# Five summed pairs per chunk instead of four in the up projection of a float32 decoder layer, one weight sum by accumulating DMA

## The reference

```
D_MODEL, SEQ, D_FF, FFN_RES_WEIGHT = 2048, 256, 5632, 0.5

def swiglu(x, wg, wu, wd):
    return (jax.nn.silu(x @ wg) * (x @ wu)) @ wd

f = swiglu(rmsnorm(h, ffn1_pre_g[l]), ffn1_wg[l], ffn1_wu[l], ffn1_wd[l])
h = h + FFN_RES_WEIGHT * rmsnorm(f, ffn1_post_g[l])
u = rmsnorm(h, mix_pre_g[l])
proj = u @ w_in[l]
...
h = h + rmsnorm(mixed, mix_post_g[l])
f = swiglu(rmsnorm(h, ffn2_pre_g[l]), ffn2_wg[l], ffn2_wu[l], ffn2_wd[l])
h = h + FFN_RES_WEIGHT * rmsnorm(f, ffn2_post_g[l])
```

## Time and profile before

| | |
|---|---|
| median of three runs | 2065.04 us (2064.78 to 2065.18) |
| profiled execution | span 2063.8 us, first to last instruction; no other time of this execution is given |
| TensorE busy | 2050.5 us, 99% of the span |
| VectorE busy | 1813.9 us, 88% |
| ScalarE busy | 1152.8 us, 56% |
| GpSimd busy | 27.7 us, 1% |
| granted TensorE clock | 0.999 of full speed over the span |
| DMA | 409.51 MB, 198 GB/s; loads on SyncE's queue take 60.4% of the 16 engines' time |

### The profile page before, as it was taken

One profiled execution on the slowest core, in us unless ns is written; L12 is line 12 of the kernel. 1 busy time (PEld: TensorE's weight loads), 2 busy tenths in 40 slices (PEclk: granted clock), 3 DMA queues, 4 the chain that ended last, 5 costly groups with the idle time before them and its releaser, 6 DMA issues.

```text
span 2063.8 us, 26172 instructions
## 1 busy us (share of the span) xinstructions
PE 2050.5 (99%) x9238; PEld 1694.8 (82%) x9238; DVE 1813.9 (88%) x2227; ACT 1152.8 (56%) x1292; POOL 27.7 (1%) x54
## 2 busy tenths in 40 slices
PE   9999999999999999999999999999999999999998
PEld 8888888888888788888788888888888888888886
DVE  7999999999888858998687566879999999999797
ACT  6565665566555554444466444565656565665463
POOL 0000000000000000100000000000000000000000
PEclk9999999999999999999999999999999999999999
DMA  8666656655666666776555566566666666646564
GB/s 327 222 207 203 202 187 212 211 164 177 201 194 205 187 186 192 208 202 183 178 169 181 181 191 213 183 233 201 198 205 208 198 203 201 206 143 207 198 208 163
DMA packets 211996, 409.51 MB, mean 198 GB/s; under 512 B 15113, under 2 KB 15377, under 8 KB 211520
## 3 DMA queue, kind: packets, MB, share of 16 engines
q1 hardware_dynamic: 209904, 401.26, 60.4%
q0 software_dynamic: 1856, 7.01, 1.5%
q10 hardware_dynamic: 144, 0.04, 0.0%
HBM read 406.14 MB, written 2.11 MB: 198 GB/s over the span
## 4 chain that ended last, share of the span: by engine, by line
PE 98%; DVE 1%; ACT 0%; issue 0%; DMA 0%; POOL 0%; DVEq 0%; SPq 0%; ACTq 0%; POOLq 0%
PE banks L1731 96%; PE banks L1781 2%; DVE wlo L1059 0%; DVE res L1114 0%; DMA raw<-in_ffn_wg_dram 0%; DVE h_lo L1349 0%; ACT act_hi L579 0%; DVE act_lo L1127 0%; ACT h_hi L767 0%; POOL stat L476 0%; ACT comb L683 0%; DVE comb L1083 0%; ACT junk L644 0%; ACT whi L564 0%; PE banks L2028 0%
## 5 line engine op out<-in xcount | busy, mean ns | idle before, releaser
L564 ACT ACTIVATE whi<-raw 128x1024 fp32r<-128x1024 f32 x579 | 597.8, 1052 | 490.2 <-PE banks L1731 298.3
L1059 DVE TENSOR_TENSOR wlo<-raw,whi 128x1024 fp32r<-128x1024 f32 x580 | 690.6, 1217 | 154.4 <-ACT whi L564 152.2
L1731 PE MATMUL banks<-whi,act_hi 128*128 128x512 f32 x1568 | 507.8, 395 | 0.7 <-DVE wlo L1059 0.7
L1731 PE MATMUL banks<-whi,act_lo 128*128 128x512 f32 x1568 | 498.2, 389 | 0.0
L1731 PE MATMUL banks<-wlo,act_hi 128*128 128x512 f32 x1568 | 485.2, 389 | 0.3 <-DVE wlo L1059 0.3
L1731 PEld LDWEIGHTS banks<-whi,act_lo 128*128 128x128 f32 x1568 | 294.3, 188 | 62.1
L1731 PEld LDWEIGHTS banks<-wlo,act_hi 128*128 128x128 f32 x1568 | 294.3, 188 | 62.0 <-DVE wlo L1059 0.7
L1731 PEld LDWEIGHTS banks<-whi,act_hi 128*128 128x128 f32 x1568 | 291.1, 188 | 62.5 <-issue 4.7
L564 ACT ACTIVATE whi<-raw_deep 128x1024 fp32r<-128x1024 f32 x176 | 183.0, 1054 | 172.4 <-DVE raw_deep L1259 156.3
L1059 DVE TENSOR_TENSOR wlo<-raw_deep,whi 128x1024 fp32r<-128x1024 f32 x176 | 207.8, 1220 | 7.0 <-ACT whi L564 6.9
L1731 PE MATMUL banks<-whi,h_hi 128*128 128x512 f32 x536 | 172.9, 390 | 0.5 <-ACT whi L564 0.5
(11 more groups left out here) (305 smaller groups left out, 2392.6 us busy)
## 6 DMA issues: line engine op xcount, KB each, us to landing
raw<-in_ffn_wd_dram SPq DMA_DIRECT2D x176, 512.0 KB, 4.7
raw<-in_w_in_dram SPq DMA_DIRECT2D x160, 512.0 KB, 3.6
raw<-in_ffn_wg_dram SPq DMA_DIRECT2D x88, 512.0 KB, 3.7
raw_deep<-in_ffn_wg_dram SPq DMA_DIRECT2D x88, 512.0 KB, 3.7
raw<-in_ffn_wu_dram SPq DMA_DIRECT2D x88, 512.0 KB, 4.7
raw_deep<-in_ffn_wu_dram SPq DMA_DIRECT2D x88, 512.0 KB, 4.5
raw<-in_w_out_dram SPq DMA_DIRECT2D x32, 512.0 KB, 4.1
raw<-in_w_pw_dram SPq DMA_DIRECT2D x16, 512.0 KB, 4.0
```

Of the source, the lines that this page charges most:

```text
L564: nc.scalar.activation(whi[:, j % RING, 0:kts * width], src[:, 0:kts * width], ACT.Copy).then_inc(hi_ready, 1)
L1059: nc.vector.tensor_tensor(wlo[:, j % RING, 0:n], raw_slot(j, deep)[0][:, 0:n], whi[:, j % RING, 0:n], ALU.subtract).then_inc(lo_ready, 1)
L1731: return nc.tensor.matmul(o, a, b, **kw)
```

## The change

1. `SEVEN` becomes (1, 2, 3, 5, 6): pair 2 of each summed chunk is a summed pair too. With it come a fifth activation sum per FFN and a fifth set of weight sums per chunk.
2. In the up projection b12+b22 is no longer made by VectorE. GpSimd waits for the slab of `wu` to land and issues a DMA that reads its second row block from DRAM once more and adds it to the first in place (`pair_sums`, `accum_op=ALU.add`, 256 KB). ScalarE's high part of slab 2q+1 and VectorE's sums wait for that DMA (`pair_added`).
3. The weight sums, with other signs, are b11-(b12+b22) in one instruction, and both other tiles (that plus b21, that plus b22) in one instruction of 128x1024 (`sums_of_lower_rows`). In the down projection b12+b22 stays on VectorE and now comes first; ScalarE waits for that one alone.
4. In chunks 1 to 10 the low parts of both slabs of a pair are one instruction of 128x2048 (`lo_pair`) that waits for both high parts.
5. GpSimd's program holds the fifty DMAs of an FFN's up projection ahead of the load of the gains (`load_gpost`) of FFN 1 and behind it in FFN 2.

```
-SEVEN = (1, 3, 5, 6)
+SEVEN = (1, 2, 3, 5, 6)
-P_SUM, R_SUM, Z_SUM = range(3)
+Z_SUM, P_SUM, R_SUM = range(3)
...
+            def pair_sums(f):
+                def one(c, group):
+                    for q in SEVEN:
+                        slab, full = raw_slot(2 * q + 1, True)
+                        pool.wait_ge(full, 16 * loads_in_up(f, c, 2 * q + 1))
+                        pool.dma_start(slab[:, 0:CW], rows(w_up[f][1])[:, 2 * q + 1, bass.ts(c, CW)],
+                                       accum_op=ALU.add).then_inc(added(f, c, q)[0], 16)
+                summed_chunks(pool.Fori, one)
...
                         hi_at(2 * q)
                         if q in SEVEN:
-                            act.wait_ge(wsum_ready, 4 * seven + 3)
+                            act.wait_ge(*added(f, c, q))
                         hi_at(2 * q + 1)
...
+            def lo_pair(j, ready):
+                dve.wait_ge(hi_ready, ready)
+                s = j % RING
+                src = raw[:, s:s + 2, :] if j % DEEP < RING else raw_deep[:, s:s + 2, :]
+                nc.vector.tensor_tensor(wlo[:, s:s + 2, :], src, whi[:, s:s + 2, :], ALU.subtract).then_inc(lo_ready, 2)
...
-                    nc.vector.tensor_tensor(wsum[:, P_SUM, :], b11, b12, ALU.add).then_inc(wsum_ready, 1)
+                    nc.vector.tensor_tensor(b12, b12, b22, ALU.add).then_inc(wsum_ready, 1)
                     dve.wait_ge(wsum_ready, 4 * seven + 1)
-                    nc.vector.tensor_tensor(wsum[:, R_SUM, :], wsum[:, P_SUM, :], b22, ALU.add).then_inc(wsum_ready, 1)
-                    nc.vector.tensor_tensor(b12, b12, b22, ALU.add).then_inc(wsum_ready, 1)
+                    nc.vector.tensor_tensor(wsum[:, R_SUM, :], b11, b12, ALU.subtract).then_inc(wsum_ready, 1)
                     dve.wait_ge(wsum_ready, 4 * seven + 2)
-                    nc.vector.tensor_tensor(wsum[:, Z_SUM, :], wsum[:, R_SUM, :], b21, ALU.add).then_inc(wsum_ready, 1)
+                    sums_of_lower_rows(n - 1, deep).then_inc(wsum_ready, 2)
+
+                def up_weight_sums(c, q, seven, opens):
...
+                    b11, b21, b12q, b22 = halves
+                    dve.wait_ge(*added(f, c, q))
+                    nc.vector.tensor_tensor(wsum[:, R_SUM, :], b11, b12q, ALU.subtract).then_inc(wsum_ready, 2)
+                    dve.wait_ge(wsum_ready, 4 * seven + 2)
+                    sums_of_lower_rows(2 * q, True).then_inc(wsum_ready, 2)
...
-                        for j in 2 * q, 2 * q + 1:
-                            lo(j, n0 + j + 1, deep=True)
+                        lo_pair(2 * q, n0 + 2 * q + 2)
```

More of the change, by code:

```diff
@@ L266, in build @@
             sem("wsum_ready"), sem("wsumhi_ready"), sem("wsumlo_ready"), sem("wsum_used"))
+        pair_added = [sem(f"pair_added{i}") for i in range(RING)]
         outer_copied, combined, silu_ready, hidden_ready = (
@@ L345, in summed_chunks, with added @@
             one(SUMMED, 0)
+        def added(f, c, q):
+            i = (2 * q + 1) % DEEP // 2
+            per_chunk = sum((2 * n + 1) % DEEP // 2 == i for n in SEVEN)
+            so_far = sum((2 * n + 1) % DEEP // 2 == i for n in SEVEN if n <= q)
+            return pair_added[i], 16 * (per_chunk * SUMMED * f + per_chunk * (c - 1) + so_far)
         def raw_slot(j, deep):
@@ L481, in _ @@
             root(1, rstd)
-            pool.wait_ge(mm_done, UP_SLABS)
+            def pair_sums(f):
[6 more added lines that the diff above has]
+                summed_chunks(pool.Fori, one)
+            pair_sums(0)
             load_gpost(f1_post)
@@ L541, in _ @@
             root(7, rstd)
+            pair_sums(1)
             root(8, rpost[0])
@@ L736, in quad @@
                     if q in SEVEN_OF[half]:
-                        act.wait_ge(wsum_ready, 4 * seven + 3)
+                        act.wait_ge(wsum_ready, 4 * seven + 1)
                     hi_at(n + 1)
@@ L1219, in act_sums @@
                     link(nc.vector.tensor_tensor(asum[:, i, S5, :], a21, a22, ALU.subtract))
[L1220 removed]
+                    nc.vector.tensor_tensor(asum[:, i, S7, :], a21, a11, ALU.subtract)
                     link(nc.vector.tensor_tensor(asum[:, i, S6, :], asum[:, i, S5, :], a11, ALU.subtract))
@@ L1244, in hidden, with sums_of_lower_rows @@
                     ins.then_inc(hidden_ready, 1)
+                def sums_of_lower_rows(n, deep):
+                    s = n % DEEP if deep else n % RING
+                    two = raw[:, s:s + 2, CW:2 * CW] if s < RING else raw_deep[:, s - RING:s - RING + 2, CW:2 * CW]
+                    return nc.vector.tensor_tensor(wsum[:, Z_SUM:P_SUM + 1, :], wsum[:, R_SUM:R_SUM + 1, :].to_broadcast([P, 2, CW]),
+                                                   two, ALU.add)
                 def weight_sums(seven, loads, j, opens, deep=False):
@@ L1255, in weight_sums @@
                     b11, b21, b12, b22 = halves
-                    nc.vector.tensor_tensor(wsum[:, P_SUM, :], b11, b12, ALU.add).then_inc(wsum_ready, 1)
+                    nc.vector.tensor_tensor(b12, b12, b22, ALU.add).then_inc(wsum_ready, 1)
                     dve.wait_ge(wsum_ready, 4 * seven + 1)
-                    nc.vector.tensor_tensor(wsum[:, R_SUM, :], wsum[:, P_SUM, :], b22, ALU.add).then_inc(wsum_ready, 1)
-                    nc.vector.tensor_tensor(b12, b12, b22, ALU.add).then_inc(wsum_ready, 1)
+                    nc.vector.tensor_tensor(wsum[:, R_SUM, :], b11, b12, ALU.subtract).then_inc(wsum_ready, 1)
                     dve.wait_ge(wsum_ready, 4 * seven + 2)
-                    nc.vector.tensor_tensor(wsum[:, Z_SUM, :], wsum[:, R_SUM, :], b21, ALU.add).then_inc(wsum_ready, 1)
+                    sums_of_lower_rows(n - 1, deep).then_inc(wsum_ready, 2)
+                def up_weight_sums(c, q, seven, opens):
+                    if not opens:
+                        dve.wait_ge(wsumlo_ready, seven)
+                    halves = []
+                    for n in 2 * q, 2 * q + 1:
+                        slab, full = raw_slot(n, True)
+                        dve.wait_ge(full, 16 * loads_in_up(f, c, n))
+                        halves += slab[:, 0:CW], slab[:, CW:2 * CW]
+                    b11, b21, b12q, b22 = halves
[3 more added lines that the diff above has]
+                    sums_of_lower_rows(2 * q, True).then_inc(wsum_ready, 2)
                 def weight_sums_lo(seven, low=wsum_lo):
@@ L1291, in summed @@
                         if q in SEVEN:
-                            weight_sums(seven, loads_in_up(f, c, 2 * q), 2 * q, first and f == 0 and q == SEVEN[0], deep=True)
+                            up_weight_sums(c, q, seven, first and f == 0 and q == SEVEN[0])
                         if q == SEVEN[0] and not first:
                             combine_last(c - 1, 1 - group, n0)
-                        for j in 2 * q, 2 * q + 1:
-                            lo(j, n0 + j + 1, deep=True)
+                        lo_pair(2 * q, n0 + 2 * q + 2)
                         if q == 6 and not first:
```

8 lines of the change are left out of this document (4 added, 4 removed).

## The result

The changed kernel takes 2114.8 us (median of 4 runs, 2114.4 to 2115.1), the kernel before 2065.1 beside it: a ratio of 1.024, 95% interval 1.0227 to 1.0252. It is slower, within the forecast range (2082 to 2116) but near its upper end, and some 15 us beyond the number forecast.

What follows compares the result with a forecast made beforehand. TensorE sets the pace now, with VectorE nearly full; after the change late low parts cost 29.9 us over 18 periods plus 4.8 in chunk 1, so 2063.8 + 34.7 = 2098.5 of span, 2099 us forecast, range 2082 to 2116.

Steps and rivals of the forecast that it cites:

- The bound: Whole kernel before the change: TensorE, busy 99% of the span, sets the pace; VectorE is busy 88%.
- the part on TensorE: One pair per summed chunk goes from 5.45 to 4.76 us: 0.69 saved in each of 20 chunks, 13.8 us.
- VectorE's prices: Times assumed for VectorE's instructions in a summed chunk, adding up to 41.91 us against today's period of 41.70.
- The chain: From TensorE's end with pair 6 through VectorE: low parts late in pairs 2 and 3, period 41.70 to 43.36 us.
- none in pairs 5, 6: Summed chunks: TensorE waits for low parts in pairs 2 and 3 (about 1.0 and 1.1 us), not in 5 and 6.
- T: TensorE's end with pair 6, at 211.78 in the earlier trace, from which the forecast counts a chunk's times.
- A: The forecast itself, low parts late in pairs 2 and 3: 2099 us, range 2088 to 2110; chance 0.80.
- C: Rival: the accumulating DMA takes 12 us to land instead of 7.7, 30 us on top, 2129; chance 0.10.
- B: Rival: VectorE's own work is the bound, its wait at `combine` doesn't tie it to TensorE: 2074 us; chance 0.05.
- the lock: At `combine`: VectorE can't work ahead, since it waits for TensorE's end with pair 6 through two ScalarE copies.

## Why the prediction was right in direction and 15 us short

**The bound and the part on TensorE** held: pairs 4 to 6 take 14.97, as forecast for one plain and two summed pairs.

**VectorE's prices** were each near, most of them a little low: 128x2048 takes 2.21 from start to start (231.94 to 234.15) for 2.20, the sums 0.78 + 1.15 = 1.93 for 1.87, the low part of the sums 1.84 where sums follow (234.15 to 235.99) for 1.79. Over a chunk they add up to the 42.73 above, where 41.91 was forecast.

**The chain** held as a mechanism: the waits in pairs 2 and 3, and the return through `wsum_hi`, are there, and the smaller ScalarE instruction showed that it lies on the path. The forecast had VectorE and ScalarE arrive together at the low part of pair 2's sums; in the trace ScalarE comes 0.30 later, which is one reason why VectorE's part could be cut without effect.

**The step that was mis-sized** is the period: "none in pairs 5, 6" and no other wait, 1.66 longer. Measured from `combine` to `combine` it is 2.28 in the first FFN (41.69 to 43.97) and 2.39 in the second. What is missing is the wait in pair 7, a term that the sum put at nothing. I took the merged low parts as a saving of 0.07 and looked for their delay in pairs 1 to 3 alone, but pair 7's also follow a wait for TensorE: low part of pair 6's sums at 218.66 (after 0.70 for ScalarE), low parts of pair 7 at 220.63 (after 0.21 for the second slab's high part), ready at 222.92. TensorE wants them 0.90 after its start, at 222.54. The trace of before held it, in VectorE's 210.48 and in ScalarE's high parts of the two slabs:

```profile
208.68 1.99 ACT L564 ACTIVATE whi<-raw_deep 128x1024 fp32r<-128x1024 f32 x2
```

They end at 210.67; one instruction that waits for both, 0.10 later and 2.29 long as in the trace after, ends at 213.06, where TensorE at 211.78 + 0.90 wants it at 212.68. Pair 7 then ends 0.56 later, so does pair 1: at T + 17.10, not T + 16.54. The low part of pair 2's sums starts at T + 18.88, not T + 18.33, and pair 3 goes on at T + 25.01, not T + 24.53; the way from there to pair 6's end is 18.95, not 18.83, which makes the 0.60 by which the period was missed. The wait alone is not all of it: VectorE could have come to that low part at T + 18.49 (237.93 + 2.20), not the T + 18.31 forecast, so that without the wait the cycle would be some 0.4 shorter (an estimate, against 240.52), and the other 0.2 are VectorE's low prices. The kernels with four pairs, where TensorE sets the time, with and without the merged instruction, price the same wait at 0.57.

**The sum of the miss**: 18 x 0.60 = 10.8; the second FFN's longer period 9 x 0.11 = 1.0; chunk 1 was 3.1 and 3.2 longer in place of 2.4 (first `combine` at 91.11, before 88.02), 1.5; after the last chunks some 0.5 in each FFN, 1.0; the median 1.6 above the span, not 1.2. Together 14.7 of 15.1. The second FFN's 0.11 is gone without the accumulating DMAs and the waits for them (nine periods from 1471.11 to 1866.80, 43.97 each); whether it is the wait or the landing stays open. It is 1 us in all, too little to be told from none in the time of that run.

**Luck.** The forecast's own range for its chain, A, ended at 2110. The time lies above it and inside the wider range only because that had room for part of the way to C, which played no part.

**The rivals.** B had its condition wrong, the lock exists. With the low parts apart it comes true in the first FFN, but at 42.88 a chunk, not 41.91. C is excluded by the run without the DMA. Beside VectorE's additions here the issue took 0.87, where the one of the earlier trace rows took 0.53, and the landing 5.7; VectorE's addition beside the issue at 230.11 took its usual 2.28 (229.75). The time was the same without the DMAs, so no run here shows a cost. Where VectorE did take longer, in the kernel with the sums on GpSimd, it stood beside GpSimd's own additions: 5.65 for 2.38 in two low parts.

**Signs forecast**: waits of some 45 us were 69.8 for weight loads and 43.6 for matmuls; a period of 43.4 with 1.4 idle was 43.96 with 1.22 idle, at the low parts of pair 2's and pair 6's sums and of pair 7, not at `combine`.

## What to carry to other kernels

Where two engines are both full, follow each buffer that only one of them may hold at a time (here one `wsum_hi`) around its cycle, at the place where the work comes in a run. The sum of an engine's work, read from start to start, is only the least that a chunk can take (here 42.73); the lock comes on top (1.22), and a mean over chunks says less still. An instruction that does two pieces of work in one is shorter, but its first piece is ready only with its last and it starts only when both inputs are there; here each saved VectorE 0.07, and all of them cost TensorE 0.57 a chunk in the kernel with four pairs. Ask of every merged instruction who wanted the first half.

## What the runs showed of the hardware

An accumulating DMA of 256 KB landed in 5.7 us at the median (a plain one in 5.6), GpSimd's issue took 0.87, and 100 of them left the time as it was (2114.8 and 2114.2). In the kernel with the sums on GpSimd a 128x1024 addition took 3.2 on GpSimd (249.54 and 255.12) against 1.23 on VectorE in the changed kernel. VectorE's low part of 128x1024, with two SBUF sources and 1.22 at the median, took 3.41 beside the first of them (at 250.41) and up to 3.43 in that run, while the 128x2048 addition with one source in PSUM beside the second took 2.27 (at 255.99), against 2.28 in the changed kernel. In the changed kernel with pair 4, TensorE's granted clock was 1.00 from 214 to 216.7, in a stall of 2.19 that ended at 216.80, and 0.50 from about 218 to 221, where matmuls started 0.43 apart instead of 0.23; behind the stall of 2.08 that ended at 262.37 it was 1.00.
